# A two-block transformer on one core: 4,096 bytes per partition of SBUF pass from the arena to the DMA descriptor scratch

## What is computed

```python
def reference(x, ...):
    x = first_block(x, c, ...)           # 2 layers
    return second_block(x, c_2, ctx_2, c_ctx_2, ...)   # 2 layers, with 256 context tokens

# first_block, each layer l
mod = silu(c) @ ada_w[l] + ada_b[l]      # shifts, scales, gates of 3 sublayers
x = layer_norm(ALPHA * x + 0.5 * gate * swiglu_ffn(modulate(x), ffn1_w_in, ffn1_w_out))
x = layer_norm(ALPHA * x + gate * (mamba2 | forgetting attention | short conv)(modulate(x) @ mix_w_in) @ mix_w_out)
x = layer_norm(ALPHA * x + 0.5 * gate * swiglu_ffn(modulate(x), ffn2_w_in, ffn2_w_out))

# second_block, layer i: GQA attention for i = 0, MLA attention for i = 1, then square(relu(h @ w1)) @ w2
x = layer_norm_2(alpha * x + g_a * mixer(x, ctx))
x = layer_norm_2(alpha * x + g_m * sq_relu_mlp(modulate(x), mlp_w1, mlp_w2))
```

## Time and profile before

| | before |
|---|---|
| timed runs | 3905.97, 3904.21, 3897.63 us |
| median | 3904.21 us |
| profiled execution, its own time | 3905.97 us |
| profiled execution, span from first to last instruction | 3904.2 us |
| mean granted TensorE clock | 0.981 |
| TensorE busy | 96% of the span |
| DMA traffic | 417.43 MB, mean 107 GB/s |

### The profile page before, as it was taken

How to read it: one execution, slowest core, us unless ns; L and a number is a source line. 1 busy time by engine, 2 the same in 40 slices (tenths; PEclk the granted TensorE clock), 3 DMA queues, 4 the chain that set the end, 5 groups by cost and what they waited for, 6 DMA issues and landing times.

```text
span 3904.2 us, 49772 instructions
## 1 busy us (share of the span) xinstructions
PE 3766.3 (96%) x19930; PEld 3185.0 (82%) x19930; DVE 2366.0 (61%) x2973; ACT 1724.5 (44%) x2636; POOL 576.7 (15%) x559
## 2 busy tenths in 40 slices
PE   8999999999999999999998989989999999999998
PEld 6888877888888888788877778888888887888886
DVE  4555776644564667777435489675555467866335
ACT  2444334443443544436332178444544245853223
POOL 1000401300130022140014200150000241113001
PEclk7999999999999999999998999989999999999999
DMA  4554211334344432135322011213332112322221
GB/s 181 209 215 164 91 65 69 148 144 179 135 161 150 181 108 78 43 108 207 127 70 88 11 29 29 84 55 130 130 122 105 49 54 69 69 73 87 97 97 65
DMA packets 71652, 417.43 MB, mean 107 GB/s; under 512 B 8976, under 2 KB 12176, under 8 KB 30480
## 3 DMA queue, kind: packets, MB, share of 16 engines
q1 hardware_dynamic: 70176, 408.20, 29.5%
q10 hardware_dynamic: 1264, 6.29, 0.4%
HBM read 393.49 MB, written 2.10 MB: 101 GB/s over the span
## 4 chain that ended last, share of the span: by engine, by line
PE 81%; DVE 13%; ACT 2%; issue 2%; POOL 2%; DMA 0%; DVEq 0%; ACTq 0%; POOLq 0%
PE ps L2000 25%; PE ps L2001 24%; PE ps L2002 24%; DVE nmax L3762 2%; DVE w_lo L2803 1%; PE ps L2697 1%; DVE gp_lo L3779 1%; POOL sq_h_lat L1090 1%; DVE x_lat L3130 1%; DVE rstd_lat L3119 1%; DVE mp_lo L3779 1%; DVE gprob L3774 1%; PE ps L2228 1%; DVE x_lat L3141 1%; DVE h_lo L3149 1%
## 5 line engine op out<-in xcount | busy, mean ns | idle before, releaser
L2000 PE MATMUL ps<-h_hi,w_lo 128*128 128x512 f32 (+2 forms) x2872 | 1084.0, 377 | 40.9 <-DVE h_lo L3149 19.8
L2002 PE MATMUL ps<-h_hi,w_hi 128*128 128x512 f32 (+2 forms) x2872 | 1069.2, 372 | 0.0
L2001 PE MATMUL ps<-h_lo,w_hi 128*128 128x512 f32 (+1 forms) x2800 | 1043.5, 373 | 0.0
L2803 DVE TENSOR_TENSOR w_lo<-raw,w_hi 128x2048 fp32r<-128x2048 f32 (+3 forms) x262 | 557.9, 2130 | 647.8 <-ACT w_hi L1296 647.6
L1296 ACT ACTIVATE w_hi<-raw 128x2048 fp32r<-128x2048 f32 (+3 forms) x262 | 457.6, 1747 | 951.8 <-PE ps L2002 940.7
L2000 PEld LDWEIGHTS ps<-h_hi,w_lo 128*128 128x128 f32 (+1 forms) x2872 | 545.7, 190 | 148.2 <-DVE h_lo L3149 24.0
L2002 PEld LDWEIGHTS ps<-h_hi,w_hi 128*128 128x128 f32 (+1 forms) x2872 | 545.4, 190 | 95.8
L2001 PEld LDWEIGHTS ps<-h_lo,w_hi 128*128 128x128 f32 x2800 | 532.1, 190 | 88.9 <-issue 0.5
L2000 PE MATMUL ps<-hid_hi,w_lo 128*128 128x512 f32 (+1 forms) x1272 | 489.7, 385 | 16.8 <-DVE w_lo L2803 10.5
L2001 PE MATMUL ps<-hid_lo,w_hi 128*128 128x512 f32 (+1 forms) x1272 | 483.9, 380 | 0.0
L2002 PE MATMUL ps<-hid_hi,w_hi 128*128 128x512 f32 (+1 forms) x1272 | 483.5, 380 | 0.0
(11 more groups left out here) (494 smaller groups left out, 6157.9 us busy)
## 6 DMA issues: line engine op xcount, KB each, us to landing
raw<-ada SPq DMA_DIRECT2D x114, 1024.0 KB, 4.9
raw<-ffn_in SPq DMA_DIRECT2D x87, 1024.0 KB, 6.8
raw<-mlp_in SPq DMA_DIRECT2D x32, 1024.0 KB, 4.9
raw<-mlp_out SPq DMA_DIRECT2D x32, 1024.0 KB, 4.9
raw<-ffn_out SPq DMA_DIRECT2D x32, 768.0 KB, 4.4
raw<-ffn_out SPq DMA_DIRECT2D x32, 640.0 KB, 3.9
raw<-mix_p SPq DMA_DIRECT2D x14, 1024.0 KB, 4.9
raw<-mix_x SPq DMA_DIRECT2D x8, 1024.0 KB, 4.9
```

Of the source, the lines that this page charges most:

```text
L2000: eng.matmul(out, lo_w, hi_x, start=first, stop=False, skip_group_check=True)
L2001: eng.matmul(out, hi_w, lo_x, start=False, stop=False, skip_group_check=True)
L2002: return eng.matmul(out, hi_w, hi_x, start=False, stop=last, skip_group_check=True)
L2803: eng.tensor_tensor(w_lo[:, slot, 0:ln.width], raw[:, slot, 0:ln.width], w_hi[:, slot, 0:ln.width].bitcast(F32), ALU.subtract).then_inc(s_ ...
```

## The change

Three numbers change, and nothing else:

```diff
@@ -283,9 +283,9 @@
     with ExitStack() as ctx:
-        arena_bytes = 225088
+        arena_bytes = 220992
         arena = ctx.enter_context(nc.sbuf_tensor("arena", [P, arena_bytes // 4], F32))
-        base = 4224
+        base = 8320
         used = {}
@@ -326,7 +326,7 @@
         psumr = place("psumr", [P, HEADS], F32, after("nmax"))
-        ctx0 = (after("psumr") + 4 * SEQ - 1) // (4 * SEQ) * 4 * SEQ
+        ctx0 = (after("psumr") + 63) // 64 * 64
         x_ctx = place("x_ctx", [P, DC, CTX], F32, ctx0)
@@ -4005,7 +4005,7 @@
-    nc = bacc.Bacc("TRN2", target_bir_lowering=False, num_devices=1, dynamic_dma_scratch_size=4096)
+    nc = bacc.Bacc("TRN2", target_bir_lowering=False, num_devices=1, dynamic_dma_scratch_size=8192)
```

## The result

| | before | after |
|---|---|---|
| median of five runs | 3904.21 us | 3922.03 us |
| lowest and highest | 3897.37, 3905.97 us | 3919.62, 3929.44 us |
| profiled execution, its span | 3904.2 us | 3928.7 us |
| mean granted TensorE clock | 0.981 | 0.98 |

The changed kernel takes 1.0053 times the time of the one before, with a 95% interval of 1.004 to 1.0067. That is 17.8 us of medians. It lies outside the 0.2% that the forecast of 3904 us allowed, and above the 3912 us at which its range ended.

A forecast was written before the change was run, and what follows sets the result against it. The prediction took the rate at which TensorE starts matmuls, with VectorE steps between stages, to bound the kernel. Its terms, 0 + 0 + 0 + 0, left the median at 3904 us, range 3894 to 3912 us.

The forecast's parts named there:

- the addresses that TensorE reads: Matmuls on hid, 3,480 of them, whose operand distance changes by 1,408 bytes: claimed 0, bounds -7 and +7 us.
- moving operand and weights collide: Slower rival: reads of hid slowed by the new distance to the weight load, 15 us more, 3919 us; chance 0.05.
- Its point of decision: Cost per hid matmul from which the slower case would be told from no change: 7.8 us / 3,480 = 2.2 ns.
- The chance of 0.07 for slower: Whole kernel slower by over 0.2%: 0.05 for colliding operand reads plus 0.02 for TensorE's clock falling elsewhere.
- The scratch: Store for descriptors that an engine's program writes; claimed unused by this kernel at either size, 0 us.
- The rival of its timed preparation: Outside the span: preparing the larger scratch is timed, +1.8 us, 3906 us; chance 0.02.
- The other engines: Operand addresses of VectorE, ScalarE and GpSimd: claimed 0, VectorE's ends -3 and +3 us, the others under 1 us.
- The addresses that DMAs write: Loads into moved tiles, slabs at the start included: claimed 0, ends none lost and 8.0 us gained.
- The 1.6% that the prediction estimated: Slab loads at the start: rows now on a 256-byte boundary, 256 beats instead of 260; sum left at 0.
- The clock: Rival: TensorE's half-speed stretches fall elsewhere, not by the change, 3896 or 3912 us; chance 0.05, of which 0.03 down.

The follow-up runs named there:

- the scan: Small kernel of TensorE alone on constant data, widths of 512 to 128 columns at distances 0, 64, 128, 192 between moving operand and weights; at 128 columns the cost is 1 ns.

## Why the prediction was wrong

**The step that failed** is "the addresses that TensorE reads", taken at 0 with ends at -7 and +7 us. It measured +19 to 21 us: from starts, 18.2 us for `hid`, 1.0 us for `y` and 0.2 us for `cqn`, two groups that the working left out. By shown means it is 6 ns x 3,480 = 20.9 us.

The working saw the right quantity. It wrote that the distance between `hid` and the weights changes by 1,408 bytes, in 3,480 matmuls. It then took rows as evidence that could not bear on it. These were `h` and `hid` at an equal 389 ns, "at very different addresses", the equal windows, and `gprob` and `mprob` at 276 and 277 ns. The addresses differ by tens of kilobytes, but the distances do not differ mod 256, because the upper part was rounded to 2,048 bytes: moving operand less weights is 0 for `h` and `hid` alike, and `ident` (byte 121,312) lies 96 mod 256 from `gprob` (190,592) and from `mprob` (98,432) alike. Each comparison was one case measured twice. The prediction saw this limit for VectorE ("upper and lower tiles both began 128 bytes past a multiple of 2,048 before") and did not put it to TensorE, where the time was. In addition, `gprob` has 128 columns, a width at which the scan shows 1 ns.

The ends failed for the same reason. They came from 392 against 390 ns, a spread among matmuls of one distance, and could not bound what another distance costs. Since no row had the new distance, the term needed a wider end, such as the 13 ns that the rival used. (The range had a slip besides: its terms together reached 3914 us, and it ended at 3912.)

**The rival that happened** is "moving operand and weights collide", at a chance of 0.05. It forecast 3919 us; the median is 3922.03. Its point of decision, 2.2 ns for each `hid` matmul, was passed with 6 ns. That its time came so close is luck: it put 13 ns on one of each three matmuls, and in fact all three have about 6 ns. Its 13 ns came from `y_hi` with `w_lo` at 403 ns, which was not the dearest 512-column form (`cqn_hi` with `w_lo` had 448) and no cost of an address: `y` stood at distance 0 before and ran at 226.8 ns by starts. Its two signs in the profile after, `hid` above `h` in mean and fewer than 440 matmuls in a window of `ffn_out`, both came: 396 against 392 ns, and 435. The chance of 0.07 for slower rested on the blind evidence too.

By the Trainium skill, TensorE: Matmul & The Clock Gate, section "Step-by-step: what each phase is for", TensorE has two independent read ports, one for the streaming operand and one for weight loads, and loading the next weights takes no read bandwidth from the running matmul. The runs here do not show the ports, but they put a condition beside that sentence: with no other engine and no DMA at work, the pitch is 227.1 or 232.5 ns by the distance between the two operands alone.

**The scratch**, taken at 0, was right within what the runs can tell: 3920.76 us (ratio 1.0048 [1.0032, 1.0065]) with 4,096 bytes and 3922.03 (1.0053 [1.004, 1.0067]) with 8,192 at the same addresses, and 1.0006 [0.9997, 1.0015] with the large scratch at distance 0. The rival of its timed preparation has no sign either: 3930.47 - 3928.7 = 1.8 us lie outside the span, as before.

**The other engines**, 0 with ends at 3 us, was right: 2289 ns for line 2899 and 683 ns for `gp_lo` again, and VectorE's busy time 0.6 us lower.

**The addresses that DMAs write**, 0, was right. The same pieces stand at the start of after's chain:

```profile
0.81 4.74 DMA x_lat<-xT
...
29.21 24.95 PE ps L2228 x128
```

They were 4.76 and 24.70 us, and `swaps` is 3.22 us where it was 3.25. The slabs landed, in median, after 24.1 us (ScalarE's queue) and 22.2 us (SyncE's) in place of 24.2 and 22.4. That is no gain by alignment: over all kernels of this document the four with slabs on a 256-byte boundary have 24.0 to 24.4 and 22.2 to 22.8 us, the five without 24.1 to 24.3 and 22.4 to 22.5. The 1.6% that the prediction estimated would have been up to 0.4 us, and no such gain shows.

**The clock** stood at 0.98 and 0.981, and equal work at equal clock had another duration, so that rival is not the cause. Its rows were misread in one point: at 52 to 56 us TensorE is shown busy for all 4.00 us; only at 2116 to 2120 us, with 2.78 us, did it idle in part.

**Not shown:** why the chip does this. In most `ffn_out` stages of after the pitch alternates between 229 and 238 ns, where it was 226 or 227 before, which looks like two streams of reads that meet at some of the starts. That is argued only. Nor is it shown why the `mks` products do not follow the distance.

## What to carry to other kernels

When a change moves tiles, write down for each pair of operands that are read together how far apart they lie, modulo small powers of two, before and after. Rows of before are evidence only if one of them has the new remainder. If none has it, the price is unknown, not zero, and multiplied by thousands of matmuls in a kernel that TensorE bounds, a few ns count. For back-to-back 128x128 by 512-column float32r matmuls, keep moving tile and weights at a multiple of 256 bytes from each other: here that gave back the 0.5%, and it took the place of two small vectors. For 256 columns it is not the best place.

## What the runs showed that I had not expected

- The pitch of 512-column matmuls with a weight load each depends on (moving - weights) mod 256: 227.1 ns at 0, 229.2 at 64, 232.5 at 128, 233.3 at 192, and up to 239.9 in steps of 4 bytes.
- Neither operand's own place matters: both moved by 640 bytes together gave 0.9998 [0.9987, 1.0009].
- With 256 columns the order turns: 119.8 ns at distance 0 (and at 96), and 117.8 to 118.6 at 64, 128 and 192.
- Shifting only the low weights or only the low moving tile gives 229.6 to 233.3 ns, at 64 bytes more than shifting both moving tiles.
